# One change in three places of a two-block transformer kernel: the attention core's order of scores and turnings, its maxima and its scale; the loads and steps of the last norm; and how the engines leave a block

## The reference, cut to what matters

```python
def attend(q, k, v):
    sm_scale = MLA_QK ** -0.5
    def one_block(qi):
        s = jnp.einsum('bqhd,bkhd->bhqk', qi, k).astype(jnp.float32) * sm_scale
        p = jax.nn.softmax(s, axis=-1).astype(v.dtype)
        return jnp.einsum('bhqk,bkhd->bqhd', p, v)
```

## Time and profile before

| | us |
|---|---|
| median of 3 runs | 4868.43 (4864.16 to 4889.18) |
| the profiled execution, its time | 4883.45 |
| its span | 4881.6 |
| TensorE busy in the span | 4242.7 (87%) |
| core of layer 0, first scores to last | 599 to 969 |
| core of layer 1 | 1586 to 1914 |
| last norm, first load issued to the end | 4793.8 to 4881.6 |

### The profile page before, as it was taken

One profiled execution on the slowest core, in us unless ns is written; L12 is line 12 of the kernel. 1 busy time (PEld: TensorE's weight loads), 2 busy tenths in 40 slices (PEclk: granted clock), 3 DMA queues, 4 the chain that ended last, 5 costly groups with the idle time before them and its releaser, 6 DMA issues. The chain is left out here.

```text
span 4881.6 us, 68841 instructions
## 1 busy us (share of the span) xinstructions
PE 4242.7 (87%) x28006; PEld 2450.6 (50%) x28006; DVE 2002.0 (41%) x4096; ACT 1338.1 (27%) x3105; POOL 518.7 (11%) x560
## 2 busy tenths in 40 slices
PE   5999799999997999999997745788698799999990
PEld 2455466644444665454556534677585344344340
DVE  1641656611715664322006667666346222222223
ACT  2111645511015554111014354333032111111111
POOL 0000000000000000000010001222002322323220
PEclk9999889999998999999997867988898899999995
DMA  5011100030111003412111020000304679999974
GB/s 190 22 60 43 36 14 14 30 131 20 56 51 36 14 14 121 164 43 74 43 65 40 2 96 6 3 3 3 113 1 159 231 255 308 311 315 352 335 244 125
DMA packets 152451, 505.37 MB, mean 104 GB/s; under 512 B 22609, under 2 KB 79554, under 8 KB 138690
## 3 DMA queue, kind: packets, MB, share of 16 engines
q1 hardware_dynamic: 114898, 379.89, 20.9%
q0 software_dynamic: 37232, 120.99, 9.0%
HBM read 402.42 MB, written 98.42 MB: 103 GB/s over the span
## 5 line engine op out<-in xcount | busy, mean ns | idle before, releaser
L697 PE MATMUL banks<-arena 128*128 128x512 f32 (+1 forms) x2928 | 1108.2, 540 | 16.6 <-DMA arena<-in_w_in 10.8
L697 PEld LDWEIGHTS banks<-arena 128*128 128x128 f32 x2928 | 559.6, 191 | 563.5 <-issue 522.8
L3146 PE MATMUL banks<-arena 128*32 128x512 f32 (+2 forms) x2896 | 561.2, 595 | 3.2 <-DMA arena<-in_experts 2.4
L884 PE MATMUL banks<-arena 128*128 128x256 f32 (+1 forms) x1152 | 378.0, 483 | 21.4 <-DMA arena<-y_d 14.6
L1269 PE MATMUL banks<-arena 96*128 96x512 f32 (+1 forms) x800 | 379.4, 558 | 11.3 <-ACT arena L1372 9.6
L3146 PEld LDWEIGHTS banks<-arena 128*32 128x32 f32 (+2 forms) x2896 | 198.7, 130 | 356.7 <-issue 354.0
L1319 DVE TENSOR_REDUCE arena<-banks 128x1 f32<-128x512 f32 (+1 forms) x400 | 238.3, 596 | 244.5 <-PE banks L1269 242.9
L884 PEld LDWEIGHTS banks<-arena 128*128 128x128 f32 x1152 | 223.0, 195 | 167.5 <-issue 147.7
L3165 PE MATMUL banks<-arena 128*32 128x512 f32 (+2 forms) x1448 | 286.4, 595 | 1.7 <-DVE arena L3195 1.2
L1277 PEld LDWEIGHTS banks<-arena 128*128 128x128 f32 x1312 | 172.7, 144 | 155.1 <-issue 123.3
L3113 POOL DMA_INDIRECT r_d<-arena x125 | 181.5, 1452 | 639.0 <-DVE arena L3195 505.8
(11 more groups left out here) (505 smaller groups left out, 5649.2 us busy)
## 6 DMA issues: line engine op xcount, KB each, us to landing
arena<-in_experts SPq DMA_DIRECT2D x64, 3072.0 KB, 13.1
arena<-in_ada_w SPq DMA_DIRECT2D x12, 2048.0 KB, 7.5
arena<-in_w_in SPq DMA_DIRECT2D x19, 1024.0 KB, 5.7
arena<-in_w_mod SPq DMA_DIRECT2D x8, 2048.0 KB, 18.4
arena<-in_w_in SPq DMA_DIRECT2D x7, 2048.0 KB, 9.3
arena<-in_w_out SPq DMA_DIRECT2D x6, 2048.0 KB, 11.1
arena<-in_w_mod SPq DMA_DIRECT2D x8, 1024.0 KB, 5.0
arena<-r_d SPq DMA_DIRECT2D x16, 512.0 KB, 5.4
```

The costliest lines, as they stand in the source:

```text
L697: i = e.matmul(self.out_of(n), lhs, rhs, start=k == 0, stop=k == KT - 1)
L884: i = e.matmul(bank(n % 4)[:, 0:nn], w[:, q, :], H[:, q, t0:t0 + nn], start=q == 0, stop=q == KT - 1)
L3146: op = e.matmul(ABK[(q - q0) % 2][rows, :], xT[(q - q0) % 2][:, P * k:P * k + P][:, rows], weights[:, i % SLOTS, 512 * k:512 * k + 512], s ...
```

## The change

It has these parts:

1. On TensorE all scores of item `n+1` come one behind the other, then all turnings of item `n`.
2. On ScalarE the copy of part 2 of item `n-1` moves between the first and the second exponential of item `n`; the copy of part 0 stays behind the exponentials.
3. The query scale is multiplied by `-SM` once a layer, on VectorE (96x1 numbers, after a wait for its load). The scores are then negative: maxima become minima, the exponential has scale -1, and one instruction joins the three minima, where there were two for the maxima. An item with one part needs none, where there was one.
4. The last norm has eight buffers for each half, so that all 16 loads are issued at once, in the order blocks 0 and 1, weight and bias, blocks 2 to 7. ScalarE does the root alone. VectorE does subtract-mean-times-weight and scale-plus-bias as two `scalar_tensor_tensor` of 128x1024.
5. The skipped block is made with `no_gpsimd_drain=True`. The language's note on it: the closing barrier goes by semaphores only and does not drain GpSimd's DMA generation.

```diff
+            e.wait_ge(*ld.at(S, "w64", "q"))
+            e.tensor_scalar(scale_of["q"], scale_of["q"], -SM, None, ALU.mult).then_inc(Vn.hit("scaling"), 1)
...
-                ahead = parts(n + 1) if n + 1 < N else []
-                for q in range(3):
-                    if q < len(ahead):
-                        scores(n + 1, *ahead[q])
-                    if q < len(parts(n)):
-                        turned(n, *parts(n)[q])
+                for part in parts(n + 1) if n + 1 < N else []:
+                    scores(n + 1, *part)
+                for part in parts(n):
+                    turned(n, *part)
...
-                    e.tensor_reduce(c[:, q:q + 1], bank(q)[:, 0:P * jn], AX.X, ALU.max).then_inc(Vn.hit(), 1)
-                    if q == 1:
-                        e.wait_ge(*Vn.own())
-                        e.tensor_tensor(c[:, 0:1], c[:, 0:1], c[:, 1:2], ALU.max).then_inc(Vn.hit(), 1)
...
+                    o = q if np_ > 1 else 3
+                    e.tensor_reduce(c[:, o:o + 1], bank(q)[:, 0:P * jn], AX.X, ALU.min).then_inc(Vn.hit("max", n), 1)
+                if np_ > 1:
                     e.wait_ge(*Vn.own())
...
-                    e.tensor_scalar(c[:, 3:4], c[:, 0:1], c[:, 2:3], -SM, ALU.max, ALU.mult).then_inc(Vn.hit("max", n), 1)
+                    e.scalar_tensor_tensor(c[:, 3:4], c[:, 0:1], c[:, 1:2], c[:, 2:3], ALU.min, ALU.min).then_inc(Vn.hit("max", n), 1)
...
+                    e.activation(pr[n % 2][:, P * j0:P * (j0 + jn)], bank(q)[:, 0:P * jn], ACT.Exp, bias=c[:, 3:4], scale=-1.0, accum_out=c[:, 4 + q:5 + q]).then_inc(Sn.hit("exp", n, q), 1)
+                    if q == 0 and n and len(parts(n - 1)) == 3:
+                        copied(n - 1, *parts(n - 1)[2])
+                copied(n, *parts(n)[0])
+            if len(parts(N - 1)) == 3:
+                copied(N - 1, *parts(N - 1)[2])
...
-        with nullcontext(Dry()) if dry else nc.Block() as block:
+        with nullcontext(Dry()) if dry else nc.Block(no_gpsimd_drain=True) as block:
...
-        rr, r1, rs = ([low(1024) for _ in range(3)] for _ in range(3))
+        rr, r1 = ([low(1024) for _ in range(8)] for _ in range(2))
...
-                e.wait_ge(*Sn.at("normed", i))
-                e.tensor_tensor(rs[i % 3], rs[i % 3], w2r, ALU.mult).then_inc(Vn.hit(), 1)
-                e.wait_ge(*Vn.own())
-                e.tensor_tensor(rs[i % 3], rs[i % 3], b2r, ALU.add).then_inc(Vn.hit("done", i), 1)
...
+                e.wait_ge(*Sn.at("root", i))
+                e.reciprocal(sd[:, i:i + 1], sd[:, i:i + 1]).then_inc(Vn.hit(), 1)
+                e.scalar_tensor_tensor(r1[i], rr[i], mv[:, 2 * i:2 * i + 1], w2r, ALU.subtract, ALU.mult).then_inc(Vn.hit(), 1)
+                e.wait_ge(*Vn.own())
+                e.scalar_tensor_tensor(r1[i], r1[i], sd[:, i:i + 1], b2r, ALU.mult, ALU.add).then_inc(Vn.hit("done", i), 1)
```

More of the change, by code:

```diff
@@ L1177, in prep_scalar @@
             yield
-            if n < 2:
-                e.wait_ge(*ld.at(S, "w64", kind))
+            if kind == "q":
+                e.wait_ge(*Vn.at("scaling"))
+            elif n < 2:
+                e.wait_ge(*ld.at(S, "w64", "k"))
             for g in range(2):
@@ L1371, in core_scalar @@
                         e.wait_ge(*Tn.at("turn", n - 2, q))
-                    e.activation(pr[n % 2][:, P * j0:P * (j0 + jn)], bank(q)[:, 0:P * jn], ACT.Exp, bias=c[:, 3:4], scale=SM, accum_out=c[:, 4 + q:5 + q]).then_inc(Sn.hit("exp", n, q), 1)
-                for q, j0, jn in parts(n):
-                    if q != 1:
-                        e.wait_ge(*Tn.at("turn", n, q))
-                        if n >= 4:
-                            e.wait_ge(*Tn.at("value", n // 2 - 2))
-                        e.activation(ptr[n % 4][:, P * j0:P * (j0 + jn)], bank(3 + q)[:, 0:P * jn], ACT.Copy).then_inc(Sn.hit("turn", n, q), 1)
+                    e.activation(pr[n % 2][:, P * j0:P * (j0 + jn)], bank(q)[:, 0:P * jn], ACT.Exp, bias=c[:, 3:4], scale=-1.0, accum_out=c[:, 4 + q:5 + q]).then_inc(Sn.hit("exp", n, q), 1)
[4 more added lines that the diff above has]
+                copied(N - 1, *parts(N - 1)[2])
         core_sync(sp), core_tensor(pe), core_vector(dve), core_scalar(act)
@@ L3287, in rows @@
             def rows(i):
-                if i >= 3:
-                    e.wait_ge(*Vn.at("done", i - 3))
                 for n, half in enumerate((rr, r1)):
                     ld.turn(e)
-                    e.dma_start(half[i % 3], r_d[n][P * i:P * i + P, :]).then_inc(ld.hit("end", "r", n, i), 16)
+                    e.dma_start(half[i], r_d[n][P * i:P * i + P, :]).then_inc(ld.hit("end", "r", n, i), 16)
             rows(0), rows(1)
@@ L3296, in end_sync @@
             row_bcast(e, b2r, A["ln2_b_2"][0], "end", "b")
-            rows(2)
+            for i in range(2, 8):
+                rows(i)
             for i in range(8):
@@ L3300, in end_sync @@
                 ld.turn(e)
-                e.dma_start(out[0][P * i:P * i + P, :], rs[i % 3]).then_inc(ld.hit("end", "out", i), 16)
-                if i + 3 < 8:
-                    rows(i + 3)
+                e.dma_start(out[0][P * i:P * i + P, :], r1[i]).then_inc(ld.hit("end", "out", i), 16)
         def end_vector(e):
@@ L3309, in stats @@
             def stats(i):
-                r = rr[i % 3]
+                r = rr[i]
                 e.wait_ge(*ld.at("end", "r", 0, i))
                 e.wait_ge(*ld.at("end", "r", 1, i))
-                e.tensor_tensor(r, r, r1[i % 3], ALU.add).then_inc(Vn.hit(), 1)
+                e.tensor_tensor(r, r, r1[i], ALU.add).then_inc(Vn.hit(), 1)
                 e.wait_ge(*Vn.own())
@@ L3320, in stats @@
                 e.tensor_scalar(sd[:, i:i + 1], mv[:, 2 * i + 1:2 * i + 2], 1.0, 1e-5, ALU.mult, ALU.add).then_inc(Vn.hit("var", i), 1)
-            def scale(i):
-                e.wait_ge(*Sn.at("root", i))
-                e.reciprocal(sd[:, i:i + 1], sd[:, i:i + 1]).then_inc(Vn.hit(), 1)
-                e.wait_ge(*Vn.own())
-                e.scalar_tensor_tensor(nb[:, i:i + 1], mv[:, 2 * i:2 * i + 1], -1.0, sd[:, i:i + 1], ALU.mult, ALU.mult).then_inc(Vn.hit("scale", i), 1)
             def last(i):
@@ L3331, in last @@
                     e.wait_ge(*ld.at("end", "b"))
-                e.wait_ge(*Sn.at("normed", i))
-                e.tensor_tensor(rs[i % 3], rs[i % 3], w2r, ALU.mult).then_inc(Vn.hit(), 1)
+                e.wait_ge(*Sn.at("root", i))
+                e.reciprocal(sd[:, i:i + 1], sd[:, i:i + 1]).then_inc(Vn.hit(), 1)
+                e.scalar_tensor_tensor(r1[i], rr[i], mv[:, 2 * i:2 * i + 1], w2r, ALU.subtract, ALU.mult).then_inc(Vn.hit(), 1)
                 e.wait_ge(*Vn.own())
-                e.tensor_tensor(rs[i % 3], rs[i % 3], b2r, ALU.add).then_inc(Vn.hit("done", i), 1)
-            for i in range(10):
+                e.scalar_tensor_tensor(r1[i], r1[i], sd[:, i:i + 1], b2r, ALU.mult, ALU.add).then_inc(Vn.hit("done", i), 1)
+            for i in range(9):
                 if i < 8:
                     stats(i)
-                if 1 <= i < 9:
-                    scale(i - 1)
-                if i >= 2:
-                    last(i - 2)
+                if i:
+                    last(i - 1)
         def end_scalar(e):
             Tn, Vn, Sn, Gn = points("end")
-            for i in range(9):
-                if i < 8:
-                    e.wait_ge(*Vn.at("var", i))
-                    e.activation(sd[:, i:i + 1], sd[:, i:i + 1], ACT.Sqrt).then_inc(Sn.hit("root", i), 1)
-                if i:
-                    p = i - 1
-                    e.wait_ge(*Vn.at("scale", p))
-                    if p >= 3:
-                        e.wait_ge(*ld.at("end", "out", p - 3))
-                    e.activation(rs[p % 3], rr[p % 3], ACT.Identity, bias=nb[:, p:p + 1], scale=sd[:, p:p + 1]).then_inc(Sn.hit("normed", p), 1)
+            for i in range(8):
+                e.wait_ge(*Vn.at("var", i))
+                e.activation(sd[:, i:i + 1], sd[:, i:i + 1], ACT.Sqrt).then_inc(Sn.hit("root", i), 1)
         end_sync(sp), end_vector(dve), end_scalar(act)
```

12 lines of the change are left out of this document (7 added, 5 removed).

## The result

The changed kernel takes 4818.55 us (median of 4, 4809.61 to 4829.94); four runs of the kernel before have a median of 4873.07 us. The two medians differ by 54.5 us, a quotient of 0.9888. The ratio on record is 0.9864, with a 95% interval from 0.9835 to 0.9894: 66 us less, between 52 and 80, which covers both figures. The forecast was 4811 us in a range from 4794 to 4832. The profiled execution took 4812.17 us with a span of 4810.3, which is 71.3 us shorter than the span of 4881.6 before.

What follows compares the result with a forecast made beforehand. TensorE, busy 87% of the span, was taken to bound the kernel outside the last norm, where VectorE waits for loads. Gains of 17 + 2 + 33 + 5.5 = 57.5 us from 4868.43 gave 4811 us, range 4794 to 4832.

Steps and rivals of the forecast that it cites:

- Scores together: Cores: all scores ahead of all turnings removes the stop inside the products; 0.27 us a pair, 17 us in all.
- new wait: Pair's first item: products start 0.19 us late, waiting for ScalarE's copy of part 0 behind the later first turning.
- The joined minima: Core, VectorE: with the vanished multiplication they shorten its chain by about 0.2 us, off the path, so no gain counted.
- The waits at the start of a core: Each layer's core start, low clock: scores' waits for the exponential, 1.36 us in layer 1, should go; 2 us together.
- the first scores of an item waiting for no exponential: Core: a sign expected in the changed profile if the forecast was right; no size given.
- The items with one part: Core, 16 items: they lose one small VectorE step, but ScalarE's copy ends close by; gain put at nothing.
- The last norm: Program's end: loads no longer wait for stores and VectorE becomes the bound at 5.81 us a block; 33 us.
- The rival in which loads share the engines and weight and bias come with the last block: Last norm: VectorE stops for weight and bias near 4822; gain 16 instead of 33 us, time 4828; chance 0.05.
- The block: Pause ahead of the last norm: ending without GpSimd's drain saves 5.5 us, bounds 0 and 6.8.
- third table load: Core, slower rival: a copy between exponentials makes ScalarE reload its function table, up to 329 us, 5140; chance 0.02.
- loss in the core: Core rival: it gives little (13 us) or a new wait eats all (0 us); 4815 to 4828; chance 0.14.
- option without effect: Block rival: the no-drain option does nothing because the engines wait for something else there; 4816 us; chance 0.05.

Runs made afterwards that it cites:

- e3: Kernel before with only TensorE's new order (all scores, then all turnings): 4891.59 us, ratio 0.9962 to the kernel before.
- e4: Kernel before with the changed query scaling, joined minima and ScalarE order, but TensorE's old order, old last norm and old block: 4896.41 us, one run.
- e5: Changed kernel with part 0's turning moved ahead of the third scores: 4812.91 us, ratio 0.9829 to the kernel before.
- e8: Kernel before with the last norm's loads all issued at once into eight buffers, its old steps kept: 4858.93 us, ratio 0.9924 to the kernel before.
- e7: The changed kernel run again, same program: 4826.39 us, ratio 0.9856 to the kernel before.
- e1: Kernel before with only the changed kernel's last norm (eight buffers, loads at once, two joined VectorE steps): 4878.05 us, ratio 0.9927 to the kernel before.
- e2: Kernel before with only the block that ends without GpSimd's drain: 4907.53 us, one run.
- e6: Kernel before with one extra, unread matmul in each one-part item of layer 0's core: 4874.52 us, one run.

## Why the prediction was right, point by point

**Scores together: right, with its new wait.** Forecast and trace: pair 9.77 and 9.78 us, first item 4.86 and 4.88, products after 3.64 and 3.63, second item 4.91 and 4.90. e3 shows that TensorE's order alone gives it, e4 that the other edits without it don't. e5 moves the copy that I named as the new wait out of the way and wins 0.18 of its 0.19 us. The layout on paper with the lags of the earlier trace rows was exact enough to design the next step from it. The forecast was 17 us in the two cores; 64 times 0.25 us are 16, and first to last copy the two layers gained 16.4.

**The joined minima: right where I forecast them, wrong where I carried them.** "The joined minima and the vanished multiplication shorten VectorE's chain by about 0.2 us" came true in the new order: 3.08 us against e3's 3.27. It cost and gave the sum nothing, since the chain is off the path there, as the prediction says. For e4 I took the same 0.2 us over to the old order, where the small step is hidden, and expected 10 to 13 us that weren't there.

**The waits at the start of a core: they shrink, they don't go.** I let the wait of the earlier trace rows go and counted 2 us for both layers. In layer 1 it fell from 1.36 to 0.70 us, 0.7 us less, so there the sign "the first scores of an item waiting for no exponential" failed. In layer 0 I tied these waits to the low clock, but they are there at the upper one too. From the first full item's first scores to its copy of part 1 it is 8.80 us in e8, which has the core of before (639.50 to 648.30), and 7.50 in the changed kernel (634.25 to 641.75), both at the upper clock: 1.3 us. At the low clock layer 0's share isn't known.

**The items with one part: nothing at the low clock, something at the upper.** I gave them nothing. At the low clock that is right: two of them take 5.48 us before (611.23 to 616.71) and 5.47 in e7 (613.90 to 619.37). At the upper clock they take 4.01 us in e8 (631.49 to 635.50) and 3.70 in the changed kernel (615.73 to 619.43), where the wait for the exponential is 0.34 instead of 0.49 to 0.52 us.

**The last norm: 33 forecast, 33.5 measured, by two errors that cancel.** A block takes 5.46 us, not 5.81: two passes in a row are 1.30 and 1.20 us apart, and the statistics of a later block take 2.89, not 2.99 us. Over seven blocks that is 2.5 us less. The first block came 7.66 us after its issue, not 5.17, 2.5 us more. e1, where the first load is as quick as before, shows the norm's own worth: 36.0 us, above the upper bound of 34 that I gave it. The rival in which loads share the engines and weight and bias come with the last block fell. But the margin is thin: the bias is there 9.9 us after its issue (4759.20), at 4769.1, and VectorE asks for it at 4769.4. In e7 it came too late by 0.17 us:

```profile
4790.02 0.16 DVE L3326 RECIPROCAL arena<-arena 128x1 f32<-128x1 f32 x1 [0.17 <-DMA arena<-in_ln_b]
```

**The block: 5.5 forecast.** The pause lost 7.2 us in the changed kernel, a little over the upper bound of 6.8, and 6.9 in e2; with the later first load it is worth 6.2 us there. The bound came from the empty DMA window, and it is this window that goes with the option: e1 still has it, the changed kernel doesn't. By the rule of the Trainium skill (Runtime: NRT & Kernel Launch, "Instruction fetch mechanics") that a branch out of the loaded pages waits for a fetch, part of the pause would stay, and 12.6 of 19.8 us did. That these are fetches isn't tested.

**The sum.** The two ends of the program took 107.6 us before and 66.9 and 66.1 us in the two profiles of the changed kernel: 41 us. With 17 us of the cores (16.4 and 0.7) it is 58 us, or 59 with the 1.3 of layer 0, for 57.5 forecast and 54.5 between the medians (66 by the ratio, 52 to 80). In e7's group the medians differ by 64.9 us (70 by the ratio, 58 to 82). So these 58 or 59 us lie at or near the lower end of both intervals, and what else the timed runs gain, if anything, isn't shown. No other rival came: no third table load, no loss in the core, no option without effect.

**What the sum left out.** The difference of 71 us between the two profiles holds some 13 us that the sum doesn't have: 16 us up to layer 0's first full item, where the clock rose early (some 3 of them are the change's at the upper clock: the 1.3 us and 0.15 us in each of eleven items with one part), 6 us between the two cores (0.7 of them the shorter wait just counted), less 8 us in the long stretch behind the cores. In that stretch all kernels here run the same instructions, and it took between 2860 and 2907 us. The stretch between the cores, with layer 1's preparation, took 622 to 627 us in the eight experiments, with no order in it by kind of kernel.

## What to carry to other kernels

When an engine is nearly always busy, lay out one period on paper with the lags read from the timeline, and look for the instruction that starts after its data, not for the share of idle time. A reordering that wins usually leaves a new, smaller wait that the same sheet of paper already shows: move that too. Compare profiles stretch by stretch before crediting a change with their difference. If one stretch gained more than its twin, run the same program again before explaining it.

## What was not expected of the hardware

TensorE left the lower clock in layer 0's core at a different moment from run to run, between about 611 and 657 us, though the instructions and their rows from 603 to 611 us were the same to 0.2 us in the changed kernel and the one before. With the same program the first full item's copy came at 641.8 and at 653.2 us; over all ten executions it came between 640.9 and 657.8. In three of them (e1, e2 and e6) the clock fell back to 1.2 GHz behind a wait of TensorE of 1.57 us and rose again some 3 to 4 us later; in e8 the same wait passed without a fall. What decides these moments stays open. Ending the block without the drain shortened the pause by 7 us but let the first load come 0.6 to 2.8 us later (5.73 to 7.66 us after its issue, for 4.87 to 5.17).
